# Neighbourhood attention, one core of Trainium2: turned exponentials stay undivided, bias and maximum share one pass

## What is computed

```python
s_lat = einsum(q, kw) * scale + bias[None]          # grid keys near the query
s_lat = where(col_ok, s_lat, NEG_INF)
s_ctx = einsum(q, kc) * scale                       # 256 context keys
p = softmax(concatenate([s_lat, s_ctx], axis=-1))
o = einsum(p_lat, vw) + einsum(p[..., kr * strip:], vc)
...
oc = context_attention(qc, kc, vc, scale)           # context queries, context keys
```

## Time and profile before

| | |
|---|---|
| runs, median of 3 | 4425.95 us (4419.4 to 4429.31) |
| the profiled execution: its time, first to last instruction | span 4426.1 us |
| PE busy, whole run | 3954.2 us (89%) |
| DVE, ACT, POOL busy | 1662.8 (38%), 1131.9 (26%), 430.0 us (10%) |
| chain that ended last: PE, transfers, DVE, ACT | 75%, 10%, 8%, 4% |
| mean granted TensorE clock | 0.931 |
| the attention stage | from 331.6 to about 560.7 us |

### The profile page before, as it was taken

How to read it: one execution, slowest core, us unless ns; L and a number is a source line. 1 busy time by engine, 2 the same in 40 slices (tenths; PEclk the granted TensorE clock), 3 DMA queues, 4 the chain that set the end, 5 groups by cost and what they waited for, 6 DMA issues and landing times.

```text
span 4426.1 us, 58380 instructions
## 1 busy us (share of the span) xinstructions
PE 3954.2 (89%) x25387; PEld 2295.7 (52%) x25387; DVE 1662.8 (38%) x3000; ACT 1131.9 (26%) x2163; POOL 430.0 (10%) x450
## 2 busy tenths in 40 slices
PE   7997897999998995478999798888989999989998
PEld 4546644333334444367898432223456754456764
DVE  2206622122124137845645412223644422654322
ACT  2114412111103256533343110001143211133211
POOL 2200011000000112301012100000002200001210
PEclk9999998999999997656797899999989999989999
DMA  6331033988973229824242399995103322112221
GB/s 239 115 122 62 18 116 136 373 323 321 361 298 138 102 82 318 266 75 117 83 128 65 148 386 409 409 409 211 43 20 121 105 78 80 41 38 95 105 77 47
DMA packets 358672, 739.07 MB, mean 167 GB/s; under 512 B 67184, under 2 KB 143456, under 8 KB 358416
## 3 DMA queue, kind: packets, MB, share of 16 engines
q1 hardware_dynamic: 348416, 697.93, 43.5%
q0 software_dynamic: 10000, 37.41, 2.4%
HBM read 673.39 MB, written 61.89 MB: 166 GB/s over the span
## 4 chain that ended last, share of the span: by engine, by line
PE 75%; DMA 10%; DVE 8%; ACT 4%; issue 1%; SPq 1%; POOL 1%; POOLq 0%; DVEq 0%; ACTq 0%
PE ps L62 73%; DMA raw<-in_moe_w_dram 7%; PE ps L66 2%; DMA b<-in_ada_w_dram 1%; DVE mx L75 1%; ACT naS L72 1%; DVE nast L90 1%; SPq L117 1%; DVE o L75 1%; DVE ps L75 1%; DMA a<-in_ada_w_dram 0%; DVE spr L75 0%; DVE sT L75 0%; DMA c<-in_w_in_dram 0%; ACT c L72 0%
## 5 line engine op out<-in xcount | busy, mean ns | idle before, releaser
L62 PE MATMUL ps<-raw,xinT 128*64 128x512 f32 (+1 forms) x4096 | 596.5, 493 | 54.4 <-DMA raw<-in_moe_w_dram 45.7
L62 PE MATMUL ps<-c,hT 128*128 128x512 f32 (+2 forms) x1024 | 419.6, 564 | 6.5 <-ACT hT L72 4.3
L62 PEld LDWEIGHTS ps<-raw,xinT 128*64 128x64 f32 (+1 forms) x4096 | 194.4, 123 | 436.8 <-issue 286.4
L62 PE MATMUL ps<-wp,hp 128*128 128x512 f32 x1536 | 361.5, 397 | 10.3 <-DVE wp L75 10.3
L62 PE MATMUL ps<-a,nahT 128*128 128x512 f32 x768 | 338.1, 597 | 5.7 <-ACT nahT L72 5.2
L62 PEld LDWEIGHTS ps<-wp,hp 128*128 128x128 f32 x1536 | 291.7, 190 | 77.5 <-DVE wp L75 10.8
L62 PEld LDWEIGHTS ps<-c,hT 128*128 128x128 f32 x1024 | 192.1, 192 | 200.4 <-issue 194.9
L62 PE MATMUL ps<-raw,hidT 128*64 128x512 f32 x1024 | 239.7, 603 | 16.8 <-DMA raw<-in_moe_w_dram 16.5
L62 PEld LDWEIGHTS ps<-a,nahT 128*128 128x128 f32 x768 | 144.1, 191 | 178.6 <-issue 177.9
L62 PE MATMUL ps<-c,oT 128*128 128x512 f32 x512 | 222.8, 592 | 1.4 <-ACT oT L72 1.4
L62 PE MATMUL ps<-xr,b 128*128 128x512 f32 (+1 forms) x432 | 161.4, 534 | 9.1 <-ACT xr L72 4.5
(11 more groups left out here) (455 smaller groups left out, 5751.7 us busy)
## 6 DMA issues: line engine op xcount, KB each, us to landing
raw<-in_moe_w_dram SPq DMA_DIRECT2D x384, 1024.0 KB, 9.9
c<-in_w_in_dram SPq DMA_DIRECT2D x28, 2048.0 KB, 9.1
a<-in_ada_w_dram SPq DMA_DIRECT2D x16, 2048.0 KB, 13.0
b<-in_ada_w_dram SPq DMA_DIRECT2D x8, 2048.0 KB, 10.5
a<-in_na_w_qkv_dram SPq DMA_DIRECT2D x6, 2048.0 KB, 18.9
c<-in_w_branch_dram SPq DMA_DIRECT2D x16, 512.0 KB, 4.1
c<-in_w_out_dram SPq DMA_DIRECT2D x4, 2048.0 KB, 9.1
c<-in_w_ple_gate_dram SPq DMA_DIRECT2D x4, 2048.0 KB, 7.8
```

Of the source, the lines that this page charges most:

```text
L62: return self.e.matmul(out, lhsT, rhs, start=start, stop=stop, skip_group_check=True) if self.e is not None else self
```

## The change

In `na_attend`:

- The exponentials are turned as they are, by TensorE's transposition mode with the identity (`e.turn`, the helper at L66). `nadiag` and its DVE instruction go; `nad` now follows the reciprocal.
- Behind the turnings, PE makes two small products per unit (stationary operand: the reciprocals of a head broadcast to 64 columns; moving operand: the identity) that lay each query's reciprocal along the columns, in bank 6 behind the fifth chunks. ACT copies bank 6 to `nafr` (384 columns for a five-chunk unit, else 128), and DVE multiplies the values' products by it on the way to `oT`, where ACT copied before.
- Bias and maximum are one DVE instruction per head for grid queries, `tensor_tensor_reduce`, with in0 the scores in PSUM, in1 the bias, out = -(scores + bias) in `naS` in SBUF, and the minimum as accumulator. The exponential then reads SBUF with scale -1. Since it covers context chunks too, the bias tile has zero chunks beside them (memsets on POOL), and in block 3 the context chunks stand first.
- The banks of a grid unit's scores count as free when DVE's passes are over (`nab`), no longer after the exponentials.
- The bias lives in slots 0 and 1 of the weight ring. POOL waits for the last ring products there, not for the fence, and each pair's bias comes in six transfers (48 in place of 8).
- The event `nat(u, 1)` follows the small products; PE waits before head 0 for ACT's copies alone, and before head 1 for DVE's alone.

```diff
+    held = len(ring.freed) - 2
+    bias = [ring.t[:, j].rearrange("p k n -> p (k n)")[:, 0:2816].rearrange("p (h t k) -> p h t k", h=2, k=128) for j in range(2)]
-    Dg = P.sb([128, 2, 2, 128], name="nadiag", ctx=d)
...
             for w in occupants(u):
-                e.wait_ge(*P.act.at('nae', w))
+                e.wait_ge(*(P.dve.at('nab', w) if units[w][1] < 4 else P.act.at('nae', w)))
...
             for h in range(2):
                 if u:
-                    e.wait_ge(*P.act.at('nat', u - 1))
-                    e.wait_ge(*P.dve.at('nat', u - 1))
+                    e.wait_ge(*(P.dve if h else P.act).at('nat', u - 1))
                 for j in range(min(n, 4)):
-                    ins = e.matmul(P.psum[:, TURN + h, j * 128:(j + 1) * 128], Sb[:, s, h, j * 128:(j + 1) * 128], Dg[:, u % 2, h, :], j == 0, True)
+                    ins = e.turn(P.psum[:, TURN + h, j * 128:(j + 1) * 128], Sb[:, s, h, j * 128:(j + 1) * 128], P.ident)
...
+            for h in range(2):
+                ins = e.matmul(P.psum[64 * h:64 * h + 64, FIFTH, 256:384], st[:, s, 2, h:h + 1].to_broadcast([128, 64]), P.ident[:], True, True)
+            ins.then_inc(*P.pe.inc('nat', u, 1))
...
-                e.activation(Sb[:, u % NS, h, 0:W], region(u)[:, h], ACT.Exp, bias=st[:, u % NS, 0, h:h + 1],
-                             accum_out=st[:, u % NS, 1, h:h + 1]).then_inc(*P.act.inc())
+                e.activation(Sb[:, s, h, 0:W], Sb[:, s, h, 0:W] if i < 4 else region(u)[:, h], ACT.Exp, bias=st[:, s, 0, h:h + 1],
+                             scale=-1.0 if i < 4 else 1.0, accum_out=st[:, s, 1, h:h + 1]).then_inc(*P.act.inc())
...
+            e.activation(FR[:, u % 2, lo:384], P.psum[:, FIFTH, lo:384], ACT.Copy).then_inc(*P.act.inc('nat', u))
...
-                if nl:
-                    e.tensor_tensor(R[:, h, 0:W], R[:, h, 0:W], bias[:, p % 2, h, bs[i]:bs[i] + nl, :].rearrange("p t k -> p (t k)"),
-                                    ADD).then_inc(*P.dve.inc())
-                    e.wait_ge(*P.dve.last())
-                e.tensor_reduce(st[:, s, 0, h:h + 1], R[:, h], AX, MAX, negate=True).then_inc(*P.dve.inc('nam', u, h))
+                if i < 4:
+                    e.tensor_tensor_reduce(out=Sb[:, s, h, 0:n * 128], in0=R[:, h], in1=bias[p % 2][:, h, bs[i]:bs[i] + n, :].rearrange("p t k -> p (t k)"),
+                                           scale=-1.0, scalar=3e38, op0=ADD, op1=ALU.min, accum_out=st[:, s, 0, h:h + 1]).then_inc(*P.dve.inc('nam', u, h))
+                else:
+                    e.tensor_reduce(st[:, s, 0, h:h + 1], R[:, h], AX, MAX, negate=True).then_inc(*P.dve.inc('nam', u, h))
...
-            e.tensor_tensor(Dg[:, u % 2], P.ident[:].unsqueeze(1).to_broadcast([128, 2, 128]),
-                            st[:, s, 2, :].unsqueeze(2).to_broadcast([128, 2, 128]), MUL).then_inc(*P.dve.inc('nad', u))
...
+        def weigh(u, p, i):
+            e.wait_ge(*P.pe.at('nao', u))
+            e.wait_ge(*P.act.at('nat', u))
+                e.tensor_tensor(dst, src.rearrange("p (r c) -> p r c", r=8), R.rearrange("p (r c) -> p r c", r=8), MUL).then_inc(*P.dve.inc('nao', u))
...
     def pool(e):
-        fence(P, e, 'na_qkv')
+        for j in range(2):
+            e.wait_ge(*P.pe.at('weights', id(ring), held + j))
+            for t in (2, 7):
+                e.memset(bias[j][:, :, t:t + 2, :], 0.0).then_inc(*P.pool.inc())
```

More of the change, by code:

```diff
@@ L84, in tensor_tensor_scan, with tensor_tensor_reduce @@
         return self.e.tensor_tensor_scan(*a) if self.e is not None else self
+    def tensor_tensor_reduce(self, **k):
+        return self.e.tensor_tensor_reduce(**k) if self.e is not None else self
     def tensor_copy(self, *a):
@@ L707, in na_attend @@
     Sb = P.sb([128, NS, 2, 640], name="naS", ctx=d)
-    PT = P.sb([128, 2, 2, 640], name="naPT", ctx=d)
-    bias = P.sb([128, 2, 2, 7, 128], name="nabias", ctx=d)
+    PT = P.sb([128, 2, 2, 512], name="naPT", ctx=d)
+    FR = P.sb([128, 2, 384], name="nafr", ctx=d)
+    held = len(ring.freed) - 2
+    assert held % ring.n == 0
+    bias = [ring.t[:, j].rearrange("p k n -> p (k n)")[:, 0:2816].rearrange("p (h t k) -> p h t k", h=2, k=128) for j in range(2)]
     st = P.sb([128, NS, 3, 2], name="nast", ctx=d)
-    Dg = P.sb([128, 2, 2, 128], name="nadiag", ctx=d)
     units = [(p, i) for p in range(8) for i in (1, 0, 3, 2, 4, 5)]
-    first = [0, 0, 1, 2, 4, 4]
-    nlat = [2, 3, 3, 2, 0, 0]
+    chunks = [(0, 1, 4, 5), (0, 1, 2, 4, 5), (1, 2, 3, 4, 5), (4, 5, 2, 3), (4, 5), (4, 5)]
     base = [0, 0, 0, 2, 0, 2]
-    bs = [0, 2, 2, 5]
+    bs = [0, 4, 4, 7]
     N = len(units)
@@ L724, in region @@
         i = units[u][1]
-        nl, step = nlat[i], 1024 if nlat[i] == 3 else 512
+        n = len(chunks[i])
+        step = 1024 if n == 5 else 512
         b0 = base[i] * 512
-        return flat[:, b0:b0 + 2 * step].rearrange("p (e w) -> p e w", e=2)[:, :, 0:nl * 128 + 256]
+        return flat[:, b0:b0 + 2 * step].rearrange("p (e w) -> p e w", e=2)[:, :, 0:n * 128]
     def occupants(u):
-        mine = lambda w: set(range(base[w], base[w] + (4 if nlat[w] == 3 else 2)))
+        mine = lambda w: set(range(base[w], base[w] + (4 if len(chunks[w]) == 5 else 2)))
         need, out = mine(units[u][1]), []
@@ L746, in in_order @@
                 weigh(u - 3, *units[u - 3])
-    def skip(*a):
-        pass
     def pe(e):
@@ L767, in turn @@
         def turn(u, p, i):
-            n, s = nlat[i] + 2, u % NS
+            n, s = len(chunks[i]), u % NS
             e.wait_ge(*P.act.at('nae', u))
@@ L818, in turned @@
             if u >= 2:
-                e.wait_ge(*P.pe.at('nao', u - 2))
+                e.wait_ge(*P.dve.at('nao', u - 2))
             e.activation(*copied(u, i, 0), ACT.Copy).then_inc(*P.act.inc())
[L821 to L824, removed]
+            e.wait_ge(*P.pe.at('nat', u, 1))
+            lo = 0 if len(chunks[i]) == 5 else 256
+            e.activation(FR[:, u % 2, lo:384], P.psum[:, FIFTH, lo:384], ACT.Copy).then_inc(*P.act.inc('nat', u))
         def turn(u, p, i):
@@ L830, in weigh @@
         def weigh(u, p, i):
[L831 to L837, removed]
+            pass
         in_order(score, turn, weigh)
@@ L888, in pool @@
                 e.wait_ge(*P.dve.at('nab', (p - 2) * 6 + 3))
-            e.dma_start(bias[:, p % 2], I['na_bias'][2 * p:2 * p + 2].rearrange("h p t k -> p h t k")).then_inc(*s_b[p % 2].inc('na', p))
+            src = I['na_bias'][2 * p:2 * p + 2].rearrange("h p t k -> p h t k")
+            for t, a, n in ((4, 2, 3), (0, 0, 2), (9, 5, 2)):
+                for h in range(2):
+                    e.dma_start(bias[p % 2][:, h, t:t + n], src[:, h, a:a + n]).then_inc(*s_b[p % 2].inc())
+            s_b[p % 2].name('na', p)
         P.end('na_attend', P.pool)
```

56 lines of the change are left out of this document (30 added, 26 removed).

## The result

| | before | changed |
|---|---|---|
| median | 4423.52 us (4 runs, 4419.4 to 4429.31) | 4360.0 us (4 runs, 4348.7 to 4362.38) |
| the profiled execution | span 4426.1 us | span 4360.7 us |
| ratio of the runs, 95% interval | | 0.9835 (0.9819 to 0.985) |
| mean granted clock, whole run | 0.931 | 0.929 |

What follows compares the result with a forecast made beforehand. The prediction took PE to bound the stage's eight pairs. Seven pairs at 7.4 us (51.8) and 14.3 for the first make 66, so 4426 - 66 = 4360 us, range 4346 to 4378, reaching to 4396 with dearer prices.

Steps and rivals of the forecast that it cites:

- The bound and the pitch: Steady pairs of the stage: PE is the bound, busy 18.7 us plus 1.0 of holes, pitch 19.7, gain 7.4 per pair.
- Turning: PE's turning of exponentials: 44 transpositions at 0.130 us replace 11.4 us of products, saving 5.7 us per pair.
- Small products: PE's new reciprocal products along the columns: 0.22 us a unit, 1.3 us more per pair.
- The dear bound of 0.58: Upper price of a unit's reciprocal products on PE: four records at a short turning's pace, 3.5 us per pair.
- Bias and maximum in one pass: DVE's pass per head: 0.95 us for five chunks, 0.80 for four; DVE busy 13.9 us per pair, covered by PE.
- The holes: PE's idle gaps, mostly before scores: 4.1 us per pair falls to 1.0 as DVE's passes release banks.
- The start: Stage's first pair: early bias brings first turning to 337.8, 10.3 us earlier, plus 4 us up to the second pair.
- The sum: Whole kernel: seven pairs at 7.4 us give 51.8, the first pair 14.3; together 66, so 4360 us.
- The clock falls: Rival, steady pairs: turnings leave PE looking idle, its work takes twice as long, about 4506 us; chance 0.03.
- DVE becomes the bound: Rival, steady pairs: DVE passes of 1.66 and 1.37 us make the pitch 23.0 and the kernel 4387 us; chance 0.10.
- The turning isn't shorter: Rival, PE's turning: a transposition might take two records, only holes close, pitch 25.4, 4402 us; chance 0.02.
- the gain doesn't reach the end: Rival, behind the stage: something waits for a transfer on its own time, kernel stays 4426 us; chance 0.02.

Runs made afterwards that it cites:

- x1_turn_by_product: The changed kernel with exponentials turned by ordinary products with the plain identity, two PE records a chunk; pitch 24.68 us, median 4394.23 us.
- x2_free_after_exp: The changed kernel with PE waiting for every unit's exponentials before overwriting banks, as before the change; pitch 22.96 us, median 4381.29 us.
- x5_small_twice: The changed kernel with each unit's two reciprocal products issued twice; pitch 20.71 us, 4363.26 us in one execution.
- x4_two_passes: The changed kernel with DVE's one pass split into an addition and a reduction; pitch 23.36 us, 4386.87 us in one execution.
- x3_late_bias: The changed kernel with POOL's memsets and bias transfers held behind the stage's opening fence; pitch 19.40 us, 4359.15 us in one execution.
- x12_changed_again: The changed kernel itself, run again on the same chip as two further steps; pitch 19.40 us, median 4355.03 us.
- x8_small_turned: The changed kernel with reciprocals written 64 times over by DVE and laid along columns by one transposition, not two products; pitch 18.60 us, median 4348.72 us.
- x11_both_copy: x10_both with DVE taking reciprocals of two columns and laying them out by a copy; pitch 18.05 us, median 4342.07 us.
- x10_both: x8_small_turned with context units also sent through the one DVE pass, so no score waits for an exponential; pitch 18.06 us, median 4345.96 us.

## Why the prediction was right

**The bound and the pitch.** Forecast: PE busy 18.7, holes 1.0, pitch 19.7, gain 7.4. Measured: 18.77, 0.63, 19.40, gain 7.73. Over seven pairs 54.1 us against 51.8.

**Turning.** Forecast 5.7 us per pair at 0.130 a record. x1_turn_by_product shows 5.28, 0.120 for each record more. The 11.39 for the products was a busy time in which the end of each group overlaps the next one, and the busy time of the turnings that replace them is 6.1 by the same count (0.139 a record), not 5.7: 0.130 came from eight in a row, while these stand in groups of four to ten, each with an end of its own. The term was mis-sized by 0.4, in the direction of less gain. PE's 18.77 met the 18.7 all the same, as closed holes took ends of groups out of the busy time (0.20 by x2_free_after_exp, for three holes). That agreement to 0.1 is luck.

**Small products.** Forecast 1.3 us per pair; x5_small_twice measured 1.31 for a set more, and by the trace after the first set costs 0.27 a unit, 1.6. The dear bound of 0.58 is excluded.

**Bias and maximum in one pass.** Forecast 0.95 for five chunks and 0.80 for four; the next head's pass starts 0.75 and 0.61 behind the first, the accumulator row overlapping. DVE is busy 12.60 us in place of 13.9. The reasoning (one column per result, as long as the reduction) held, the 0.20 of ACT's accumulator row was too much for DVE's 0.083.

**The holes.** Forecast 4.1 to 1.0; measured 0.63. x2_free_after_exp shows that 3.56 us of the gain hang on the release, and x4_two_passes that the release needs the short pass. The comparison of 2.05 us of PE work against 1.9 us of passes was close, and with 1.6 us of passes there was room. The hole that was to stay at 0.36 grew to 0.63, within the 1.0 allowed.

**The start.** Forecast turning at 337.8, 10.3 us earlier, and 4 us after it. Measured 338.90, 9.2 us, and 5.1 after it; first pair 19.62 us in place of 34.12, 14.5 against 14.3 forecast. The scores' end to the first pass took 0.34 us and not nothing, and the forecast had the second unit's scores at their usual 1.13 us, while at clock 0.50 DVE could begin its pass only 2.13 us behind their start (335.18 to 337.31). x3_late_bias puts the bias's part at 6.4 to 6.7.

**The sum.** The stage gave 69.2 us, 66 were forecast; the rest of the run gave 3.8 back in the profiled executions, which is inside its own spread. That the median met 4360.0 is therefore luck in its last digits (the same kernel came out 73.7 us under the kernel before in x12_changed_again): the gain of the stage is confirmed to about 3 us.

**The rivals.** *The clock falls*: the granted clock is 1.00 in the pair, though transpositions fill 6.1 of PE's time; by what the Trainium skill says of it ("TensorE: Matmul & The Clock Gate", Part 4: PE-mode transpose), PE would not have had the full clock for them, and the trace doesn't agree. The one stretch of the stage at 0.50 opened with scores, after PE had stood, and ended while turnings and scores ran. No run set the clock, so the rival was tested by these rows alone. *DVE becomes the bound*: not at 0.75 us a pass; x4_two_passes shows the case at its real price. *The turning isn't shorter* and *the gain doesn't reach the end*: excluded by x1_turn_by_product and by the SP issue that moved with the stage.

## What to carry to other kernels

When PE is 85% busy, look for who owns the other 15%: nearly half of this gain was holes. To close them, ask which instruction releases a PSUM bank, and how soon it is done. Moving the release without shortening the work in front of it gave 0.8 us a pair, shortening it without the move 1.2, both 4.7. Likewise cutting records alone gave 3.0, the pass with the earlier release alone 4.0, all of it 7.7. And an engine's idle share says nothing of its cover: DVE had a third of the pitch idle, yet 5.5 us more work cost 4.0.

## What the runs showed of the hardware that I had not expected

DVE's reciprocal is slow per column. For two columns it takes 0.16 us and looks free, for 128 it takes 0.947; a copy of 128 columns takes 0.227. From the block's tile in x8_small_turned, and DVE's groups in x11_both_copy:

```profile
L96 DVE RECIPROCAL narb<-nast x48: 940/947/952, 338.9 to 483.6; 128x128 f32<-128x128 f32 x48
...
L66 PE MATMUL ps<-ident,narb x48: 272/273/421, 342.2 to 485.5; 128*128 128x128 f32 x48
```

```profile
L90 DVE COPY narb<-nast 128x128 f32<-128x128 f32 x42 | 9.5, 227 | 1.5
...
L96 DVE RECIPROCAL nast<-nast 128x2 f32<-128x2 f32 x42 | 6.7, 160 | 0.0
```

(947 - 160) / 126 is 6.2 ns a column, six times the pace of the one pass, which goes from 419 ns for 256 columns to 822 for 640 in x10_both, 1.05 ns a column. The expectation of 0.29 us for it, worked out as for any pass, was wrong. The Trainium skill, "VectorE: DVE Perf Modes", First, the fixed hardware budget, says that the reciprocal is an iterative division with a repeat count of 8; the slope here agrees that a column takes several steps, at six times the pass's pace. So divide few columns and copy the result.

The fused pass with an accumulator costs one plain pass: addition, scaling, minimum and output over 640 columns in 0.822 us, while split in two instructions each of them takes 0.820.
